# Modulation sums moved into the projections, and an attention front on unscaled latents and queries, in a decoder-layer kernel

## What is computed

```python
cond = silu(c)                                        # 1024
mod = cond @ ada_w + ada_b                            # 1024 x 6144: 24 MB of weights
shift1, scale1, gate1, shift2, scale2, gate2 = split(mod, 6)
h = rms_norm(x, norm_mix_w) * (1 + scale1) + shift1
c_q, c_kv, k_rope, slab, gate_a, gate_b = split(h @ w_in, (256, 128, 32, 1792, 1024, 1024))

# attention branch, 8 heads of 64 + 32 (rope) query and key columns
q  = (rms_norm(c_q, q_a_norm_w) @ w_q_up).reshape(S, 8, 96)
kv = (rms_norm(c_kv, kv_a_norm_w) @ w_kv_up).reshape(S, 8, 128)
k_nope, v = kv[..., :64], kv[..., 64:]
k = concat(k_nope, broadcast(k_rope))
q, k = rms_norm(q, q_norm_w), rms_norm(k, k_norm_w)   # over the 96 columns of a head
q, k = rope(last 32 columns of q), rope(last 32 columns of k)
o_a = causal_softmax(q k^T / sqrt(96)) v @ w_o_mla

# recurrent branch from slab, merge with the two gates, x += gate1 * mix,
# then an expert layer on rms_norm(x, norm_ffn_w) * (1 + scale2) + shift2, x += gate2 * ffn
```

## Time and profile before

| | us |
|---|---|
| three executions | 1943.92, 1947.18, 1948.35 |
| profiled execution | 1953.72 |
| its span, first to last instruction | 1951.9 |
| first phase | 0 to 89.1 |
| projection up to k3 | 89.1 to 157.9 |
| rest of the projection | 157.9 to 223 |
| recurrent phase | 223 to 368.3 |
| attention front | 368.3 to 433.8 |
| score units | 433.8 to 492 |
| output phase, routing | 492 to 758 |
| experts | 758 to 1951.9 |

### The profile page before, as it was taken

The page is one execution under the profiler, slowest core; times in us unless marked ns, Lnnn a source line. Parts: engine busy times, 40 slices in busy tenths (PEclk is TensorE's granted clock), DMA queues, the critical chain, the costliest instruction groups (busy, mean ns, idle before and its releaser), DMA issues.

```text
span 1951.9 us, 30583 instructions
## 1 busy us (share of the span) xinstructions
PE 1817.2 (93%) x11056; PEld 1401.9 (72%) x11056; DVE 1421.0 (73%) x1609; ACT 1089.9 (56%) x1175; POOL 336.2 (17%) x248
## 2 busy tenths in 40 slices
PE   5899997659999856999999999999999999999998
PEld 2444697348478854888888888888888888888884
DVE  4516743545134546999999999999999999999994
ACT  2013322345312223777777777777777777777771
POOL 3000240120000001122131221221212212212220
PEclk9999999769999966999999999999999999999998
DMA  9920000400131216999999999999999999999996
GB/s 349 346 78 0 2 4 4 156 0 1 43 129 44 87 57 235 380 370 367 365 374 369 366 364 374 365 368 365 370 368 367 367 374 368 368 373 362 374 360 239
DMA packets 247409, 500.39 MB, mean 256 GB/s; under 512 B 14730, under 2 KB 16839, under 8 KB 246131
## 3 DMA queue, kind: packets, MB, share of 16 engines
q1 hardware_dynamic: 235108, 480.87, 68.1%
q0 software_dynamic: 9648, 17.32, 2.4%
q10 hardware_dynamic: 2592, 1.31, 0.2%
HBM read 495.76 MB, written 21.51 MB: 265 GB/s over the span
## 4 chain that ended last, share of the span: by engine, by line
PE 60%; DVE 0%; ACT 0%; ACTq 0%; issue 0%
PE bank L1806 18%; PE bank L1804 18%; PE bank L1805 18%; PE bank L1801 2%; PE bank L1819 1%; PE bank L1791 1%; PE bank L1882 1%; PE bank L1876 1%; DVE sb_e_lo L2002 0%; ACT sb_e_hi L1888 0%; DVE sb_mod L2090 0%; DVE sb_mod L2093 0%; DVE sb_x L2095 0%; ACTq L1737 0%; DVE sb_x_lo L1999 0%; ACT sb_y L1898 0%
## 5 line engine op out<-in xcount | busy, mean ns | idle before, releaser
L2002 DVE TENSOR_TENSOR sb_e_lo<-sb_w_raw,sb_e_hi 128x2048 fp32r<-128x2048 f32 x388 | 875.6, 2284 | 1.8 <-ACT sb_e_hi L1888 1.8
L1888 ACT CAST sb_e_hi<-sb_w_raw 128x2048 fp32r<-128x2048 f32 x389 | 742.7, 1910 | 82.1 <-PE bank L1806 48.8
L1804 PE MATMUL bank<-sb_e_hi,sb_x_hi 128*128 128x512 f32 x1032 | 409.7, 397 | 0.0
L1806 PE MATMUL bank<-sb_e_hi,sb_x_lo 128*128 128x512 f32 x1032 | 404.3, 392 | 0.0
L1805 PE MATMUL bank<-sb_e_lo,sb_x_hi 128*128 128x512 f32 x1032 | 403.4, 391 | 0.0
L1973 POOL TENSOR_TENSOR sb_tick<-sb_ones 128x1 f32<-128x1 f32 x64 | 158.2, 2471 | 874.5 <-DVE sb_row L2071 697.2
L1806 PEld LDWEIGHTS bank<-sb_e_hi,sb_x_lo 128*128 128x128 f32 x1032 | 194.2, 188 | 42.6
L1805 PEld LDWEIGHTS bank<-sb_e_lo,sb_x_hi 128*128 128x128 f32 x1032 | 194.6, 189 | 40.3
L1804 PEld LDWEIGHTS bank<-sb_e_hi,sb_x_hi 128*128 128x128 f32 x1032 | 194.7, 189 | 36.6
L1804 PE MATMUL bank<-sb_e_hi,sb_a_hi 128*128 128x512 f32 x512 | 205.5, 401 | 0.0
L1806 PE MATMUL bank<-sb_e_hi,sb_a_lo 128*128 128x512 f32 x512 | 200.3, 391 | 0.0
(11 more groups left out here) (398 smaller groups left out, 2447.7 us busy)
## 6 DMA issues: line engine op xcount, KB each, us to landing
sb_w_raw<-in_w_gate_up_dram SPq DMA_DIRECT2D x262, 1024.0 KB, 6.8
sb_w_raw<-in_w_down_dram SPq DMA_DIRECT2D x128, 1024.0 KB, 7.3
sb_ring<-in_ada_w_dram SPq DMA_DIRECT2D x12, 2048.0 KB, 12.2
sb_ring<-in_w_in_dram SPq DMA_DIRECT2D x7, 2048.0 KB, 9.9
sb_x<-in_x_dram SPq DMA_DIRECT2D x2, 2048.0 KB, 12.9
sb_ring<-in_w_out_dram SPq DMA_DIRECT2D x2, 2048.0 KB, 8.0
sb_e_hi<-y_rows SPq DMA_DIRECT2D x4, 1024.0 KB, 8.5
sb_e_lo<-y_rows SPq DMA_DIRECT2D x4, 1024.0 KB, 15.7
```

The lines of the kernel that those rows point to most:

```text
L1804: te.matmul(out, hi[:, k0 + k, :], w_hi, start=(first and k == 0 and what >= 2 * GU), stop=False)
L1806: mm = te.matmul(out, lo[:, k0 + k, :], w_hi, start=False, stop=(last and k == 3))
L1888: return sc.copy(g.e_hi[:, p % PARTS, :, :], raw(p))
L2002: return ve.tensor_tensor(g.e_lo[:, p % PARTS, :, :], raw(p), g.e_hi[:, p % PARTS, :, :].bitcast(F32), ALU.subtract).then_inc(split_done[p ...
```

## The change

There are two parts.

**Late modulation parts.** The first phase handles parts 0 to 3 only. Part 3 has a buffer of its own (`ada_last`), loaded without a wait. The columns of shift and scale come from 16 matmuls of one row by one column instead of 16 transposes. Features are transposed between parts 2 and 3 and are taken out of PSUM by DVE (even) and ACT (odd). The FFN norm weight isn't broadcast any more. Parts 4 to 11 are loaded in the projection as 16 halves of 1 MB into `g.x` and `g.mod` (four at a time), and DVE alone multiplies and adds all eight slices of each part: 64 operations placed behind the ten shifts. Each part's 128-partition sum is stored to DRAM (`mod_parts`), loaded back in the attention phase into GA's ring slot, summed over the partitions by one PE matmul in every third score unit (units 2, 5, up to 23), copied back by DVE, finished by POOL (times and plus the FFN norm weight) and stored to `mod_rows`. GA is loaded behind that.

**Attention front.** Latents are transposed unscaled; the norm factors are taken into the later norms' bias, the key's rope part, the values (`scale_v`) and, for queries, into the exponential's scale (`fq`). Queries and keys get their norm weights on the way out of the transposes (`wcol`), and for the rope columns through the tables. DVE ropes the queries only, the key's rope part being formed once for all heads. POOL does nothing there, and two of the four copies into `qkT` move from ACT to DVE.

Core of the diff:

```diff
@@ phase_adaln, tensor engine
+            for j in range(3):
+                modulation(j)
+            te.wait_ge(*act.at(f"xn{NT - 1}"))
+            for k in range(5):
+                features(k)
+            te.wait_ge(*act.at("mod2"))
+            features(5)
+            modulation(3)
+            te.wait_ge(*act.at("mod3"))
+            for i in range(2 * KD):
+                mm = te.matmul(ps[0][:, i:i + 1], g.mod1[0:1, i // 4, P * (i % 4):P * (i % 4) + P], g.ones[0:1, 0:1], start=True, stop=True)
...
+            features(6)
...
+            features(7)
@@ phase_adaln, scalar engine
+            for k in ks[1::2]:
+                sc.wait_ge(*pe.at(f"h{k}"))
+                sc.activation(g.hT[:, k, :], ps[bank_of[k]][:, :], ACT.Identity, bias=g.mod1_cols[:, k:k + 1], scale=g.gain[:, k:k + 1]).then_inc(*act(f"h{k}"))
@@ phase_project, where the late sums go
+        for name, n in (("l0", 2), ("l1", 6), *((f"{x}{i}", 7) for x in "rk" for i in f4)):
@@ phase_project, sync engine
+            sp.wait_ge(*vec.at("no_bias"))
+            for h in HALVES:
+                j, rows = h // 2, 512 * (h % 2)
+                if h % 2 == 0:
+                    if j >= 2:
+                        sp.wait_ge(*vec.at(f"ad{j - 2}0"))
+                    bias(j)
+                if h >= 4:
+                    sp.wait_ge(*vec.at(f"ad{j - 2}{4 * (h % 2) + 3}"))
+                sp.dma_start(staged[h % 4], ada_chunk(g.a, j + 4, rows, rows + 512)).then_inc(late_in[h % 4], 16)
+                if h >= 4 and h % 2:
+                    part(j - 2)
+                for at, chunk, last in ((5, RKV + 2, "l1"), (11, MLA, "r3")):
+                    if h == at:
+                        sp.wait_ge(*pe.at(last))
+                        load_chunk(g, sp, chunk)
+            part(LATE - 2)
+            part(LATE - 1)
@@ phase_project, scalar engine, ahead of the sigmoids
+            sc.wait_ge(*vec.at(late_ops[-1]))
@@ phase_project, vector engine
+            def late(name):
+                for n in late_at.get(name, []):
+                    j, k = int(n[2]), int(n[3])
+                    acc, before = late_acc[:, j % 2, :], bias_row[:, j % 2, :]
+                    if k % 4 == 0:
+                        h = 2 * j + k // 4
+                        ve.wait_ge(late_in[h % 4], 16 * (h // 4 + 1))
...
+                        if j >= 2:
+                            ve.wait_ge(g.parts_out[j % 2], 16 * (j // 2))
+                    ve.scalar_tensor_tensor(acc, staged[(2 * j + k // 4) % 4][:, k % 4, :], g.cond[:, k:k + 1], before, ALU.mult, ALU.add).then_inc(*vec(n))
...
@@ phase_project, vector engine, last line of shift(name, dst, mu)
+                late(name)
@@ phase_mla, tensor engine
-                te.wait_ge(*vec.at("ck3" if j == 2 else "cq3"))
-                    mm = te.transpose(ps[j][:, P * t:P * t + P], g.cn[:, t, P * j:P * j + P], g.ident[:, :])
+                    mm = te.transpose(ps[j][:, P * t:P * t + P], g.mla_in[:, t, P * j:P * j + P], g.ident[:, :])
...
+                te.matmul(ps[7][0:1, :], g.ones[:, 0:1], parts[:, j, :], start=True, stop=True).then_inc(*pe(f"md{j}"))
...
+                if u in late_after:
+                    late_sum(late_after[u])
@@ phase_mla, sync engine
+            load_chunk(g, sp, OA)
+            load_chunk(g, sp, OB)
...
+            sp.dma_start(parts, g.mod_parts.rearrange("j p n -> p j n")).then_inc(parts_in, 16)
+            sp.dma_start(ffn_row, g.a["norm_ffn_w"]).then_inc(ffn_in, 16)
+            sp.wait_ge(*pool.at("g2"))
+            sp.dma_start(g.mod_rows, mod_row).then_inc(g.mod_out, 16)
+            sp.wait_ge(g.mod_out, 16)
+            load_chunk(g, sp, GA)
@@ phase_mla, scalar engine, per tile t, behind the sine, a root (rkv) and DVE's reciprocal (sv)
+                for i in range(2):
+                    sc.wait_ge(*pe.at(f"kv{i}_{t}"))
...
+                    sc.activation(g.sqk[:, 8 + 4 * i:12 + 4 * i, 0:NOPE], kv[:, :, 0:NOPE], ACT.Square).then_inc(*act(f"kq{i}_{t}"))
+                    sc.activation(g.v_tok[:, t, 256 * i:256 * i + 256].rearrange("p (h n) -> p h n", h=4), kv[:, :, NOPE:], ACT.Copy, scale=scale_v[:, t:t + 1]).then_inc(*act(f"vv{i}_{t}"))
...
+                sc.activation(g.sqk[:, 0:HEADS, :], x[:, 0:HEADS, :], ACT.Square).then_inc(*act(f"sq{t}"))
@@ phase_mla, vector engine, per tile t
+                ve.tensor_reduce(g.ssn[:, t, HEADS:2 * HEADS], g.sqk[:, 8:16, 0:NOPE], AX_X, ALU.add).then_inc(*vec(f"red{t}"))
+                ve.wait_ge(*act.at(f"q1_{t}"))
+                for i, (n, xx) in enumerate((("c1_", x1), ("s2_", x2), ("c2_", x2), ("s1_", x1))):
+                    ve.tensor_tensor(tmp[i], xx, g.tab[:, i, t:t + 1, :].broadcast_to([P, HEADS, HALF]), ALU.mult).then_inc(*vec(f"{n}{t}"))
...
+                ve.wait_ge(*act.at(f"sk{t}"))
+                ve.reciprocal(fk, fk).then_inc(*vec(f"rk{t}"))
+                for i in range(2):
...
+                    ve.tensor_tensor(x[:, 8 + 4 * i:12 + 4 * i, 0:NOPE], kv[:, :, 0:NOPE], fk[:, 4 * i:4 * i + 4].unsqueeze(2).broadcast_to([P, 4, NOPE]), ALU.mult).then_inc(*vec(f"k{i}_{t}"))
...
+                if t:
+                    turned(t - 1)
+                    query_scale(t - 1)
+                ve.tensor_reduce(g.ssn[:, t, 0:HEADS], g.sqk[:, 0:HEADS, :], AX_X, ALU.add).then_inc(*vec(f"rq{t}"))
```

More of the change, by code:

```diff
@@ L112, in ring_chunks @@
     slab = MLA_IN
-    chunks = [rows(a["ada_w"], 512 * j, 512 * j + 512) for j in range(12)]
+    chunks = [ada_chunk(a, j) for j in range(RING)]
     chunks += [rows(a["w_in"], slab + 3 * WIDTH, slab + SLAB)]
@@ L141 @@
 PE_K = 4
+LATE = 8
 def phase_adaln(nc, g):
@@ L161, in phase_adaln @@
[L161 to L164, removed]
+        accs, js, ks = range(PE_K, KD), range(4), range(KD)
@@ new lines, in phase_adaln @@
+        vec = g.steps(ctx, "a_vec", ["rows", "cols", "cond"] + names("r{}", PE_K) + [x for j in js for x in [f"a{j}_{k}" for k in accs] + (["rstd"] if j == 2 else [])]
+                      + ["mcol", "gain"] + names("h{}", KD)[0::2])
+        act = g.steps(ctx, "a_act", ["sig", "sq0", "sq1", "sq2", "sq3", "std", "mod0", "mod1"] + names("xn{}", NT) + ["mod2", "mod3"] + names("h{}", KD)[1::2])
+        pe = g.steps(ctx, "a_pe", ["rows"] + [x for j in range(3) for x in (f"k{j}", f"p{j}")] + names("h{}", 6) + ["k3", "p3", "mcol", "h6", "h7"])
@@ L310, in _, with modulation @@
             te.wait_ge(*vec.at(f"r{PE_K - 1}"))
-            for j in range(12):
-                te.wait_ge(*chunk_loaded(g, j))
+            def modulation(j):
+                te.wait_ge(*loaded(j))
                 if j >= 3:
@@ L318, in _ @@
                 for k in range(PE_K):
-                    mm = te.matmul(out, g.rep[:, k, :], slot(g, j)[:, k, :], start=(k == 0), stop=False)
+                    mm = te.matmul(out, g.rep[:, k, :], weights(j)[:, k, :], start=(k == 0), stop=False)
                 mm.then_inc(*pe(f"k{j}"))
@@ L1011, in up @@
                     mm.then_inc(*pe(f"q{i}_{t}"))
-                for i in range(2):
-                    if t:
-                        te.wait_ge(*act.at(f"vv{i}_{t - 1}"))
-                    te.matmul(ps[2 + i][:, :], g.cT[:, 2, at], g.w_kv[:, 512 * i:512 * i + 512], start=True, stop=True).then_inc(*pe(f"kv{i}_{t}"))
+            te.wait_ge(*act.at("ct2"))
             te.wait_ge(w_in, 32)
@@ L1138, in _ @@
                 n = P * (u // HEADS + 1)
+                if u % HEADS == 0:
+                    sc.wait_ge(*vec.at(f"fs{u // HEADS}"))
                 sc.wait_ge(*vec.at(f"ng{u}"))
-                sc.activation(prob[:, u % 3, 0:n], ps[u % 3][:, 0:n], ACT.Exp, bias=negs[:, u:u + 1], scale=SCALE,
+                sc.activation(prob[:, u % 3, 0:n], ps[u % 3][:, 0:n], ACT.Exp, bias=negs[:, u:u + 1], scale=fq[:, u:u + 1],
                               accum_out=sums[:, u:u + 1]).then_inc(*act(f"ex{u}"))
```

368 lines of the change are left out of this document (215 added, 153 removed).

## The result

The changed kernel takes 1916.33 us (median of four runs, 1914.77 to 1917.0) against 1947.76 for the kernel before (four runs); the ratio is 0.9838, 95% interval 0.9822 to 0.9853. That is 31.4 us less. The prediction was 43.8 less and 1903.4, with a range that ended at 1916: the direction was right, the forecast gain was two fifths too high (43.8 against 31.4), and the result lies just outside the range.

What follows compares the result with a forecast made beforehand. Bounds were taken by stage: DMA in the first, PE in projection and score units, a hand-off chain in the front. -35.8 + 2.1 + 6.2 - 23.2 + 6.9 = -43.8, from 1947.18 to 1903.4 us; range 1892 to 1916.

Steps and rivals of the forecast that it cites:

- Score units: Units after the front: eight sums over partitions, two passes of 0.43 us each on full PE, +6.9 (6 to 10).
- First stage: Start of kernel: eight of twelve weight chunks leave the DMA-bound stage; projection starts at 53.3 instead of 89.1, -35.8.
- 1.35 us of everybody's DMA: First stage: removing the FFN norm weight's 512 KB row was taken to bring the normalised x 1.35 us earlier.
- Cold clock: Start of projection: PE, nearly idle from 45 to 53.3, runs eight passes at a lower clock, +2.1 (0 to 3.5).
- End of the projection: After the last shift DVE still has seven sums, delaying ACT's first sigmoid and the next stage, +6.2 (5.4 to 8.5).
- covered: Projection: DVE's wait on a store comes nine us after issue, against 5 to 6 for a landing, so costs nothing.
- Front: Attention front: raw latents transposed at once, cycle 7.1; first scores 42.2 us after the start instead of 65.4, -23.2.
- rival (d): Attention front: a drain of 1.4 us at each of two table switches on ACT's path, +2.8, 1906.2; chance 0.05.
- Rival (a): Attention front: cycle stays near the old 9.9 instead of 7.1, three times 2.8, 1911.8; chance 0.15.
- (b): Projection: each late multiply-add costs 0.9 us, +6.7, 1910.1; chance 0.08.
- (e): Projection: late sums starve, for instance on late halves; slower than before, 1954 at 1.6 us per multiply-add; chance 0.02.

Runs made afterwards that it cites:

- the constant: Kernel with the sums in the front and early multiply-adds, given a constant for the exponential's scale and the negated maximum: 1900.06 us in a single execution.

## Why the prediction was wrong, point by point

- **Score units, +6.9 taken, +11.5 measured: the step that failed most.** "Two passes of 0.43 each" was the busy time alone. Each sum displaces 1.04 us, the first 1.9 at the lower clock: 7 x 1.04 + 1.9 = 9.2. The other 2 came with the new front (units 60.0 in it alone): its exponential's table load stands between the first scores and the first exponential, PE idles 1.66 us for it and then runs at the lower clock. The prediction names this load but prices only the sine's and the root's. The wider exponentials are no visible part of it (the constant gave nothing back). That PE was full there, and the DVE copies hidden, was right.
- **First stage, -35.8 taken, -33.2 measured.** The failed sentence is that the 512 KB row "is 1.35 us of everybody's DMA". It went through ahead of everybody; the landing of x is the same with and without it within what the traces can tell. Another 0.6 is that the first trace of before had x at 25.61, where the later ones had 25.93 and 27.01. The chain behind x was right: 16.1 us in both traces of the changed kernel; in two of the variants, where the columns took 5.6 and 5.8 us at the lower clock, it was 17.9 and 18.1.
- **Cold clock, +2.1 taken, +3.0 measured** (71.9 and 71.7 against 68.8 for the ten features): right mechanism (with fillers ahead of them the features took 68.8 at a clock of 1.00), size within its bounds of 0 to 3.5.
- **End of the projection, +6.2 taken; +7.0 and +9.7 in the two traces** (72.1 and 74.9 us against 65.1; the first sigmoid came 6.8 and 9.0 us later than before). Right mechanism, shown by starting the multiply-adds earlier. What failed is the word "covered": the store took 8.3 and 10.5 us among the loads, and the landing of an undisturbed load had been taken for it.
- **Front, -23.2 taken, -22.3 measured.** The first scores came 41.4 and 42.5 us after the start, 42.2 predicted; the cycle was 7.2 (7.1). Here the base moves: the old front has two lengths, 3.7 apart.
- **Table loads, rival (d): fell.** In the changed kernel the sine's table load ran from 348.25 to 349.53 and its activation started at 349.55; the root's from 349.87, its activation at 351.17. The trace again has no time behind a load. The drain that the Trainium skill gives ("ScalarE: Activation LUTs", What ACT_TABLE_LOAD costs) is not seen in these two switches.
- **Rival (a), the front's cycle staying at 9.9, fell; (b), 0.9 for a multiply-add, fell** (0.75 busy, one every 0.79). (a)'s 1911.8 and (b)'s 1910.1 lay nearer the result for no reason of theirs. **(e)** had its mechanism, waits for DMA in front of the late sums, but for stores and not for halves, and at 1.3 and 4.0 us in all it was far from the 43.8 that it needed.
- **The range** let one rival at a time decide, 1911.8 at most, and its end at 1916 left 4 us beyond that. Here the units (+11.5) passed their bound of 10, the projection's end (+9.7) its bound of 8.5 in one trace, and the normalised x was 2.4 late on the mean of two traces, for which the sum had no bound at all; all in one direction.

## What to carry over

Price an instruction put on a full engine by what it displaces: from the start of its neighbour to the start of the next, at the clock that stretch really has, and not by its busy time. Bytes removed from a DMA-bound stage save time only if they moved while the engines were full: look at the window in which they moved. Before a stage's length is used as a base, or two traces are subtracted, take a second trace of the same kernel: here the unchanged recurrent phase differed by 6.1 us between three traces and the old front by 3.7, as much as the smaller terms. Where the order of an engine's stream changes, look at what used to overlap, here a table load with the first scores, and whether it still does.

## What the hardware showed unexpectedly

The recurrent phase, with the same instructions, took between 139.2 and 145.3 us in the three traces of before. The old front took 61.8 us at a granted clock of 0.75 in one trace, 65.4 and 65.5 at 0.68 in the other two. Matmuls with a weight of one row took the same 3.7 us for 32 instructions at full clock whether they moved 1 or 32 columns. A 256 KB store issued among 1 MB loads took 8.3 and 10.5 us to land. With three filler matmuls around the columns the granted clock was 0.63 from 52 to 58 us and 1.00 over all ten features behind them.
